# The merge's attention branch first, its inputs loaded and split during the convolution's last pass

## The reference, cut to what matters

```python
def _merge(z, hy_out, na_out, w_branch_hy, w_branch_na, w_out):
    a = hy_out @ w_branch_hy
    b = na_out @ w_branch_na
    g_hy = jax.nn.sigmoid(z[..., COL_G_HY:COL_G_NA])
    g_na = jax.nn.sigmoid(z[..., COL_G_NA:P_IN])
    return (g_hy * a + g_na * b) @ w_out
```

## Time and profile before

| what | value |
|---|---|
| median of 3 runs | 2767.18 us |
| lowest and highest of them | 2766.28 and 2768.03 us |
| the profiled execution, its own time | 2769.33 us |
| its span, first to last instruction | 2767.5 us |
| busy in the span: PE, DVE, ACT, POOL | 2603.5, 2202.1, 1510.9, 139.7 us |
| mean granted TensorE clock | 0.973 |
| 0 to 953 us, 954 to 1052 us | all up to the end of the convolution, the merge |

### The profile page before, as it was taken

The page is one execution under the profiler, slowest core; times in us unless marked ns, Lnnn a source line. Parts: engine busy times, 40 slices in busy tenths (PEclk is TensorE's granted clock), DMA queues, the critical chain, the costliest instruction groups (busy, mean ns, idle before and its releaser), DMA issues.

```text
span 2767.5 us, 34582 instructions
## 1 busy us (share of the span) xinstructions
PE 2603.5 (94%) x13665; PEld 2202.0 (80%) x13665; DVE 2202.1 (80%) x2033; ACT 1510.9 (55%) x1409; POOL 139.7 (5%) x159
## 2 busy tenths in 40 slices
PE   6999989989999799929999999999999999999997
PEld 2777878879998787828888888888888888888885
DVE  5674279959878656488898888888888888888887
ACT  4422146633221212237777777777777777777774
POOL 0011000000111000000000000000000000000000
PEclk9999999999999899959999999999999999999999
DMA  7598843346887763269999999999999999999994
GB/s 265 172 315 301 252 88 55 97 160 208 285 266 257 268 207 115 99 252 380 380 365 384 389 379 365 383 388 378 365 387 394 368 367 396 384 366 381 387 378 176
DMA packets 206014, 816.61 MB, mean 295 GB/s; under 512 B 31967, under 2 KB 89671, under 8 KB 127712
## 3 DMA queue, kind: packets, MB, share of 16 engines
q1 hardware_dynamic: 182228, 694.82, 67.2%
q0 software_dynamic: 23472, 119.56, 12.7%
q10 hardware_dynamic: 158, 0.07, 0.0%
HBM read 747.00 MB, written 67.39 MB: 294 GB/s over the span
## 4 chain that ended last, share of the span: by engine, by line
PE 52%; ACT 2%; issue 2%; DVE 1%; DVEq 0%; ACTq 0%
PE moe_ps_gate L2129 18%; PE moe_ps_up L2129 16%; PE moe_ps_y L2119 16%; PE moe_ps_h L2100 2%; ACT moe_w_hi L2170 1%; PE moe_ps_x L2092 1%; DVE raw L2292 0%; ACT moe_xt_hi L2163 0%; DVE moe_w_lo L2222 0%; DVE moe_h L2243 0%; ACT moe_sl L2183 0%; DVE raw L2279 0%; PE moe_ps_gate L2153 0%; PE moe_ps_gate L2155 0%; PE moe_ps_up L2153 0%
## 5 line engine op out<-in xcount | busy, mean ns | idle before, releaser
L2222 DVE TENSOR_TENSOR moe_w_lo<-raw,moe_w_hi 128x2048 fp32r<-128x2048 f32 x528 | 1207.8, 2291 | 159.7 <-ACT moe_w_hi L2170 159.1
L2170 ACT ACTIVATE moe_w_hi<-raw 128x2048 fp32r<-128x2048 f32 x528 | 1010.9, 1919 | 379.4 <-PE moe_ps_gate L2129 128.0
L2129 PE MATMUL moe_ps_up<-moe_w_hi,moe_xt_hi 128*128 128x512 f32 (+1 forms) x768 | 292.4, 381 | 0.0
L2129 PE MATMUL moe_ps_gate<-moe_w_hi,moe_xt_hi 128*128 128x512 f32 (+1 forms) x768 | 289.1, 376 | 1.4 <-DVE moe_xt_lo L2213 1.4
L2129 PE MATMUL moe_ps_gate<-moe_w_hi,moe_xt_lo 128*128 128x512 f32 (+1 forms) x768 | 286.6, 373 | 0.0
L2129 PE MATMUL moe_ps_up<-moe_w_hi,moe_xt_lo 128*128 128x512 f32 (+1 forms) x768 | 286.3, 373 | 0.0
L2129 PE MATMUL moe_ps_gate<-moe_w_lo,moe_xt_hi 128*128 128x512 f32 (+1 forms) x768 | 286.1, 372 | 0.0
L2129 PE MATMUL moe_ps_up<-moe_w_lo,moe_xt_hi 128*128 128x512 f32 (+1 forms) x768 | 285.8, 372 | 0.0
L2119 PE MATMUL moe_ps_y<-moe_w_hi,moe_ht_hi 128*128 128x512 f32 x704 | 218.7, 392 | 0.0
L2119 PE MATMUL moe_ps_y<-moe_w_lo,moe_ht_hi 128*128 128x512 f32 x704 | 217.1, 390 | 0.0
L2119 PE MATMUL moe_ps_y<-moe_w_hi,moe_ht_lo 128*128 128x512 f32 x704 | 217.0, 389 | 0.0
(11 more groups left out here) (277 smaller groups left out, 3907.2 us busy)
## 6 DMA issues: line engine op xcount, KB each, us to landing
raw<-in_w_moe SPq DMA_DIRECT2D x528, 1024.0 KB, 7.1
hyena_g_parts<-gw_d POOLq DMA_DIRECT2D x64, 1024.0 KB, 5.8
proj_w_mod<-in_w_mod SPq DMA_DIRECT2D x32, 512.0 KB, 7.5
gw_d<-proj_g_parts POOLq DMA_DIRECT2D x16, 1024.0 KB, 7.9
w_in<-in_w_in SPq DMA_DIRECT2D x12, 1024.0 KB, 7.7
norm_w_mod<-in_w_mod SPq DMA_DIRECT2D x16, 512.0 KB, 6.8
proj_g_raw<-in_w_in SPq DMA_DIRECT2D x16, 512.0 KB, 9.3
hyena_h_parts<-hq_d POOLq DMA_DIRECT2D x16, 512.0 KB, 8.2
```

Source lines behind the costliest of these rows:

```text
L2129: mm = pe.matmul(ps, hp[:, e % 2, k, :], wp[:, r, :], start=(k == 0 and x == 0), stop=(k == KD - 1 and x == 2))
L2170: act.activation(w_hi[:, g % PARTS], raw[:, g % RAW], ACT.Copy).then_inc(hi_ready, 1)
L2222: dve.tensor_tensor(w_lo[:, g % PARTS], raw[:, g % RAW], w_hi[:, g % PARTS].bitcast(F32), ALU.subtract).then_inc(lo_ready, 1)
```

## The change

- The merge's buffers and semaphores are made ahead of the convolution (`merge_places`), at addresses that its last pass does not use. The attention input has three raw slots of 512 KB.
- In `hyena`, ahead of pass 3's steps, SP issues the two weight loads of d = 0 and three pieces of the attention input. The fourth piece goes behind the last gate store.
- ACT makes `b_hi` of d = 0 ahead of block 54's sigmoid, and the high parts of attention pieces 0, 1, 2 behind the sigmoids of blocks 55, 57 and 59; that of piece 3 is its last instruction of the block.
- POOL, when its last gate weights are issued, makes `b_lo` of d = 0 and the four low parts of the attention input, by `tensor_tensor` on 128 x 1024 elements. Before, DVE made these five (L1624, L1645).
- In `merge`, only `y_t` is left to load or split for the start, and PE runs b = 1 (attention) ahead of b = 0 in d = 0.

```diff
--- before.py
+++ after.py
@@ -1124,6 +1124,9 @@
+        coming = keep["merge"]
+        branch_in, na_in, na_hi_ready, na_lo_ready, bh_ready, bl_ready = (
+            coming[n] for n in ("w_in", "na_in", "in_hi_ready", "in_lo_ready", "bh_ready", "bl_ready"))
...
@@ -1197,10 +1200,23 @@
                     sp.wait_ge(g_evacuated, n + 1)
                     sp.dma_start(g_d[n // N_BLOCKS, n % N_BLOCKS], g_out[:, n % 2]).then_inc(g_kept[n % 2], 16)
 
+                def load_na(k):
+                    s = k % NA_SLOTS
+                    if k >= NA_SLOTS:
+                        sp.wait_ge(na_lo_ready, k - NA_SLOTS + 1)
+                    sp.dma_start(coming["na_raw"][:, s], a["na_d"][k]).then_inc(na_in, 16)
+
                 load_decay(0)
                 sp.dma_start(y_t[:, 0:2], u_d[0][:, 0:2]).then_inc(v_in, 16)
                 sp.dma_start(y_t[:, 2:4], u_d[0][:, 2:4]).then_inc(v2_in, 16)
                 for p in range(-1, PASSES):
+                    if p == PASSES - 1:
+                        sp.wait_ge(tap_used, PH * PASSES)
+                        sp.wait_ge(a_done, a_at["seg", p, PH - 1] + 1)
+                        for b, w in enumerate(branch_sources(a)):
+                            sp.dma_start(coming["b_raw"][:, 0, b], w[0]).then_inc(branch_in[0], 16)
+                        for k in range(NA_SLOTS):
+                            load_na(k)
                     for r in range(PH):
                         for n in AT_SEG[p, r]:
                             keep_g(n)
@@ -1217,6 +1233,7 @@
                                 keep_g(n)
                     for n in AT_END[p]:
                         keep_g(n)
+                load_na(3)
                 for s in range(2):
                     sp.wait_ge(g_kept[s], 16 * N_G // 2)
 
@@ -1237,6 +1254,15 @@
                     pool.dma_start(g_parts[:, n % G_SLOTS], a["gw_d"][n % N_BLOCKS]).then_inc(g_in[n % G_SLOTS], 16)
                     if n == 0:
                         load_h(0)
+
+                pool.wait_ge(bh_ready, 1)
+                pool.tensor_tensor(coming["b_lo"][:, 0], coming["b_raw"][:, 0], coming["b_hi"][:, 0].bitcast(F32),
+                                   ALU.subtract).then_inc(bl_ready, 1)
+                na_hi, na_lo = coming["hi"][1], coming["lo"][1]
+                for k in range(4):
+                    pool.wait_ge(na_hi_ready, k + 1)
+                    pool.tensor_tensor(na_lo[:, k], coming["na_raw"][:, k % NA_SLOTS], na_hi[:, k].bitcast(F32),
+                                       ALU.subtract).then_inc(na_lo_ready, 1)
 
             @block.tensor
             def _(pe):
@@ -1373,10 +1399,21 @@
                     act.activation(g_out[:, n % 2], ps_g[:, n % 2, 0:QUARTER], ACT.Sigmoid, bias=par[:, b:b + 1]
                                    ).then_inc(g_evacuated, 1)
 
+                def high_na(k):
+                    act.wait_ge(na_in, 16 * max(NA_SLOTS, k + 1))
+                    act.activation(coming["hi"][1][:, k], coming["na_raw"][:, k % NA_SLOTS], ACT.Copy
+                                   ).then_inc(na_hi_ready, 1)
+
                 for p in range(-1, PASSES):
+                    if p == PASSES - 1:
+                        act.wait_ge(branch_in[0], 32)
+                        act.activation(coming["b_hi"][:, 0], coming["b_raw"][:, 0], ACT.Copy).then_inc(bh_ready, 1)
+                        act.wait_ge(out_done, NB * p)
                     for r in range(PH):
                         for n in AT_SEG[p, r]:
                             gates(n)
+                        if p == PASSES - 1 and r % 2 and r // 2 < NA_SLOTS:
+                            high_na(r // 2)
                         if p + 1 < PASSES:
                             evacuate("seg", p + 1, r)
                     for i in range(NB):
@@ -1393,6 +1430,7 @@
                             evacuate("input", q, 2 * i + 1)
                     for n in AT_END[p]:
                         gates(n)
+                high_na(3)
 
             @block.vector
             def _(dve):
@@ -1526,35 +1564,52 @@
                         transform(U_LEAF[q], U_SPEC[q], nothing)
 
 
-def merge(nc, sems, a, keep, y_t, m_t):
+NA_SLOTS = 3
+
+
+def merge_places(nc, sems):
 
     with ExitStack() as ctx:
         m = Maker(nc, ctx, "merge_")
-        in_hi, in_lo = m.sb("in_hi", [P, 2, 4, T], F32R), m.sb("in_lo", [P, 2, 4, T], F32R)
-        na_t = m.sb("na_t", [P, 4, T])
-        b_raw = m.sb("b_raw", [P, 2, 2, 4, P])
-        b_hi, b_lo = m.sb("b_hi", [P, 2, 2, 4, P], F32R), m.sb("b_lo", [P, 2, 2, 4, P], F32R)
-        gate = m.sb("gate", [P, 2, 2, T])
+        at = {"b_raw": m.sb("b_raw", [P, 2, 2, 4, P]),
+              "b_hi": m.sb("b_hi", [P, 2, 2, 4, P], F32R), "b_lo": m.sb("b_lo", [P, 2, 2, 4, P], F32R)}
+        m.sb("room", [P, PH * 2 * P])
+        at["na_raw"] = m.sb("na_raw", [P, NA_SLOTS, T])
+        hi, lo = [None, None], [None, None]
+        hi[0], hi[1] = m.sb("y_hi", [P, 4, T], F32R), m.sb("na_hi", [P, 4, T], F32R)
+        at["gate"] = m.sb("gate", [P, 2, 2, T])
+        lo[0], lo[1] = m.sb("y_lo", [P, 4, T], F32R), m.sb("na_lo", [P, 4, T], F32R)
+        at["hi"], at["lo"] = hi, lo
+    at["w_in"] = [sems(f"branch_in{s}") for s in range(2)]
+    for n in ("na_in", "in_hi_ready", "in_lo_ready", "bh_ready", "bl_ready"):
+        at[n] = sems(n)
+    return at
+
+
+def branch_sources(a):
+    return [a[n].rearrange("(k p) (d c) -> d p k c", p=P, c=P) for n in ("w_branch_hy", "w_branch_na")]
+
+
+def merge(nc, sems, a, keep, y_t, m_t):
+
+    with ExitStack() as ctx:
+        m = Maker(nc, ctx, "merge_")
+        at = keep["merge"]
+        b_raw, b_hi, b_lo, gate, in_hi, in_lo = (at[n] for n in ("b_raw", "b_hi", "b_lo", "gate", "hi", "lo"))
         ps = m.psum("ps", [P, 4, 2, 512])
 
-
-        w_in = [sems(f"branch_in{s}") for s in range(2)]
+        w_in, in_hi_ready, in_lo_ready, bh_ready, bl_ready = (
+            at[n] for n in ("w_in", "in_hi_ready", "in_lo_ready", "bh_ready", "bl_ready"))
...
@@ -1575,19 +1630,19 @@
                 def branch(s, th, b, first=False):
                     for k in range(4):
                         if first:
-                            pe.wait_ge(in_lo_ready, 4 * b + k + 1)
+                            pe.wait_ge(in_lo_ready, k + 1 if b else 4 + k + 1)
                         hi, lo = b_hi[:, s, b, k, :], b_lo[:, s, b, k, :]
                         cols = slice(th * 512, (th + 1) * 512)
                         for x, (w, h) in enumerate(((hi, in_hi), (hi, in_lo), (lo, in_hi))):
-                            mm = pe.matmul(ps[:, 2 * s + th, b, :], w, h[:, b, k, cols],
+                            mm = pe.matmul(ps[:, 2 * s + th, b, :], w, h[b][:, k, cols],
                                            start=(k == 0 and x == 0), stop=(k == 3 and x == 2))
                     return mm
 
                 pe.wait_ge(bl_ready, 3)
-                branch(0, 0, 0, first=True)
-                branch(0, 1, 0)
+                branch(0, 0, 1, first=True)
+                branch(0, 1, 1)
                 for th in range(2):
-                    branch(0, th, 1, first=not th).then_inc(branched, 1)
+                    branch(0, th, 0, first=not th).then_inc(branched, 1)
                 for d in range(1, KD):
                     s = d % 2
                     pe.wait_ge(bl_ready, d + 3)
@@ -1603,12 +1658,8 @@
                     act.wait_ge(branched, 2 * d + 2)
                     act.activation(b_hi[:, s], b_raw[:, s], ACT.Copy).then_inc(bh_ready, 1)
 
-                for b, src in enumerate((y_t, na_t)):
-                    if b:
-                        split(0, 0, 0)
-                        act.wait_ge(na_in, 64)
-                    for k in range(4):
-                        act.activation(in_hi[:, b, k, :], src[:, k, :], ACT.Copy).then_inc(in_hi_ready, 1)
+                for k in range(4):
+                    act.activation(in_hi[0][:, k, :], y_t[:, k, :], ACT.Copy).then_inc(in_hi_ready, 1)
                 with act.Fori(0, KD // 2 - 1) as i:
                     split(1, i, 2 * i + 1)
                     split(0, i + 1, 2 * i + 2)
@@ -1637,13 +1688,10 @@
                         dve.tensor_tensor(m_t[:, 2 * i + s, cols], gate[:, s, 0, cols], gate[:, s, 1, cols], ALU.add
                                           ).then_inc(merged, 1)
 
-                for b, src in enumerate((y_t, na_t)):
-                    if b:
-                        split(0, 0)
-                    for k in range(4):
-                        dve.wait_ge(in_hi_ready, 4 * b + k + 1)
-                        dve.tensor_tensor(in_lo[:, b, k, :], src[:, k, :], in_hi[:, b, k, :].bitcast(F32),
-                                          ALU.subtract).then_inc(in_lo_ready, 1)
+                for k in range(4):
+                    dve.wait_ge(in_hi_ready, 4 + k + 1)
+                    dve.tensor_tensor(in_lo[0][:, k, :], y_t[:, k, :], in_hi[0][:, k, :].bitcast(F32),
```

(2 more changed lines are left out.)

10 lines of the change are left out of this document (2 added, 8 removed).

## The result

| | before | the change |
|---|---|---|
| median, 7 runs each on one chip | 2768.03 us | 2776.97 us |
| lowest and highest | 2766.28, 2774.51 us | 2775.65, 2781.31 us |
| ratio, 95% interval | | 1.0032, 1.0021 to 1.0043 |
| the profiled execution's own time, and its span | 2769.33, 2767.5 us | 2775.65, 2773.9 us |
| TensorE clock; POOL busy | 0.973; 139.7 us | 0.973; 152.2 us |

The change costs 8.9 us in the medians, where a gain of 6.8 was forecast. The measure that I follow from here on is **the stretch** from the start of the gate block that stands ahead of `outputs(2, 0)` (at 857.31 us before, at 856.86 after) to the merge's first matmul. It is 103.4 us before and 111.6 after: 8.3 longer. What lies ahead of it differs by 0.4 us, what lies behind it by 1.4, in the change's favour.

What follows compares the result with a forecast made beforehand. PE was taken to set the merge's pace, so its start decides: 953.9 (fourth piece at 953.6 plus barrier 0.3) instead of 960.67, 6.8 us earlier. Against the median 2767.18 this gave 2760.4 us, range 2755.5 to 2767.0.

Steps and rivals of the forecast that it cites:

- First weights: Pass 3, block 56: weights land 8 us after issue, PE stands 5.4 us, and is 8.0 us late after a slow block.
- What comes back: End of pass 3: `hyena_gate` lands in 8.5 us, so block 62's 4.26 us stand and slow clock vanish, 6.9 us back.
- Start of the merge: Later of convolution's end (953.0) and fourth piece (953.6), plus the barrier's 0.3: PE starts at 953.9, 6.8 us earlier.
- What bounds the kernel: PE sets the merge's pace; a barrier follows, so an earlier merge end shortens the whole by as much.
- Rival (b): Pass 3: short-row weight loads starve, take 13.2 us, PE stands 10.6 us; 2765.6, up to 2767; chance 0.28 with (d).
- Attention input: Pass 3: three pieces land at about 922.5, bounds 916.9 and 930; the high part ends just inside the stand.
- The fourth piece: Convolution's end: load 3.5 us, ACT 1.0, POOL's subtraction 2.3 from issue at 946.8, so done at 953.6.
- Rival (d): Merge starts no earlier because POOL's last subtraction is late, which would have to take 9 us; chance 0.28 together with (b).
- Rival (c): Pass 3: ACT waits twice in full DMA; block 58 stands 7.6 us, clock 2.6, 6.9 stays; 2777.5 us; chance 0.05.
- the gap is over 9 us: Sign of a wrong prediction: PE's gap between blocks 55 and 56, expected at 3 to 7 us.
- `b_hi` at 919.12: Sign on ACT in pass 3: `b_hi` of the weights was expected at 914 to 919 us.
- `hyena_gate` at 11.3 us: Sign in pass 3: `hyena_gate` was to land in under 10 us, with no gap ahead of block 62.

Runs made afterwards that it cites:

- e11_rows: Attention first, loads behind store 61, no POOL arithmetic, but the two weight loads (512-byte rows) at the change's place, nobody waiting; ratio 0.9990 against the kernel before.
- e12_piece: Attention first, loads behind store 61, no POOL arithmetic, but one attention piece (4 KB rows) at the change's place, nobody waiting; 2764.76 us.
- e4_act: The change with ACT's four high parts (weights, pieces 0 to 2) moved behind sigmoid 61, loads left in place; ratio 1.0035 against the kernel before.
- e2_last_dve: The change with only the fourth attention piece's subtraction moved from POOL to DVE's end, four left on POOL; 2770.84 us.
- e1_dve: The change with all five subtractions moved from POOL to DVE, the fourth piece's behind the last product; 2771.29 us.

## Why the prediction was wrong

The forecast was 2760.4 with a range to 2767.0; the median is 2777.0, on the side that had a chance of 0.05. Measured in the stretch, 15.1 us lie between forecast (-6.8) and profile (+8.3), and they divide so:

| step | predicted | measured | missed |
|---|---|---|---|
| start of the stretch to the end of block 55 | 0 | -2.0 | -2.0 |
| *First weights*: blocks 56 to 61 with their stands | 8.0 - 1.0 = 7.0 | 10.6 | 3.6 |
| *What comes back*: stand and slow block 62 | 6.9 back | 4.26 - 4.15 + 5.26 - 4.43 = 0.9 back | 6.0 |
| *Start of the merge*: `outputs(3, 0)` to the first matmul | 953.9 - 941.3 = 12.6 | 20.3 | 7.7 |

The first row is mostly ahead of the change's first load (907.26): shorter waits for `h_parts` and fewer slow matmuls, not the change's doing. In the second, 10.6 is the stand of 10.33 and 18.91 us for six blocks, less about 18.6 for the same blocks before, an old stand of 1.10 included. The rows add up to 15.3; the prediction's own times for block 62, 938.4 and 941.3, give 6.6 back and not its 6.9.

**What bounds the kernel** held: the merge's start decides, and what lies behind it moved by 1.4 us, of which 0.7 is the clock (7 slow matmuls lose 1.5 us, where 12 lost 2.3).

**First weights: mis-sized.** I took 8 us for the landing, "nearer the store's row", inside bounds of 3.6 and 13.2; it was 11.4. Size was the wrong guide. With it, the load was issued 2.7 us ahead of the end of block 55, where I had 4.2. So the stand was 4.9 us longer, while the slow blocks behind it lost 1.0 less. Rival (b) had the mechanism, short rows against POOL's long ones, and e11_rows and e12_piece bear it out for the last rows of the second load; most rows did not wait so. The Trainium skill's DMA: Bandwidth & Descriptors (Queues, rings and completion order) says that each DMA engine takes turns between queues, a packet at a time; the traces agree, with the 0.34 us from one late short row to the next beside 8 KB packets of 0.33. That rival (b)'s stand of 10.6 is so near the measured 10.33 is in part luck: it had taken a landing of 13.2 and the earlier issue.

**Attention input:** "landed at about 922.5" was right: the third piece landed at 922.86, piece 0 was rounded from 922.89 on, and it stopped nothing further.

**What comes back: failed.** I argued that POOL's queue has run empty in the stand, so that `hyena_gate` lands in 8.5 us. It had, but the load came too late to use it: it was issued at 928.98, after POOL had resumed at 925.49, and took 11.3; sigmoid 60 again waited 7.34 us for a store behind it. In e4_act the stand came two blocks later. There `hyena_gate` was issued at 929.21, 3.9 us before POOL resumed, took 5.9, and this second stand was absent.

**The fourth piece: right.** From sigmoid 63: 0.9 to the issue (1.0 taken), 3.9 for the landing (3.5), 1.06, and 2.35 on POOL (2.3). The Trainium skill's GPSIMD Engine Reference (Elementwise — side-by-side cycle accounting), by whose figure I had estimated 2.25, agrees too. The Trainium skill's page SBUF — State Buffer (SBUF: two separate sides), by which a DVE operation with two SBUF inputs and a GpSimd one that reads SBUF exclude each other, is borne out: the last pair of products took 2.20 us beside POOL's subtraction and 0.76 without, and another pair 4.88 in e4_act. I had left about 1 us of it out of the sum; it was 1.4.

**Start of the merge: failed, and by most.** "The barrier's 0.3" is the barrier of a kernel whose POOL drain has ended 15.8 us earlier. With arithmetic on POOL shortly ahead of it, the barrier opens 6.6 us behind the last operation. That is 5.7 of the 7.7 us, as DVE's last product was followed by 6.6 us instead of 0.9. Of the rest 1.4 is the product beside POOL, and 0.6 a sum that was wrong on paper: I let `outputs(3, 0)` give back 0.8 us of slow clock, while it took 2.14 us and 1.95 after. Rival (d) named POOL's last subtraction as the way in which the merge starts no earlier, and asked whether the operation could take 9 us; it takes 2.35, and what follows it makes up the rest.

**Rival (c)** forecast 2777.5, and 2777.0 was measured. One of its terms is what happened: `hyena_gate` met POOL's loads, and of the 6.9 us 6.0 stayed. The rest is luck. Its largest term, a stand of 7.6 us ahead of block 58, never came, since the pieces had landed by 922.9 and not at 933; and it knew nothing of the barrier's 6.3 us.

Of the signs listed, "the gap is over 9 us" came true, and `b_hi` at 919.12, `hyena_gate` at 11.3 us and the gap ahead of block 62 missed their marks. PE's start was not near 960 either, but at 968.50.

## What to carry to other kernels

A load slipped into a full stretch is priced by its row length and by who shares the DMA engines rather than by its bytes, and it can delay the stores queued behind it, whether or not anyone waits for it. Work moved to an idle engine is priced together with what comes next on that engine, here a barrier: moving one of five operations back (e2_last_dve) or all of them (e1_dve) gave 5 to 6 us. When the time between two stands is full, an earlier load moves a stand more readily than it removes one: look for the place where the DMA is idle instead, as behind block 61.
